# A hybrid DeltaNet, Hyena and expert kernel: its long convolution in 64 real slots, its output weights, expert lists and last norm rearranged

## The chip, the cores and the metric

The kernel runs on one core of one Trainium2 chip, in one launch, with all of its data in f32. The time is that of the device, in microseconds (us), from the launch's first instruction to its last. Of the kernel before there are three timed runs: 4009.3, 4010.4 and 4012.45 us, median 4010.4. One more execution was profiled.

## What is computed

The reference is one layer over 2048 latent tokens of width 1024 and 256 context tokens. Cut to what matters:

```python
hc = rmsnorm(ctx, norm1_g) * (1 + sc1c) + sh1c
_, s_f, s_b = deltanet_branch(hc @ w_in[:, :A_COLS], lp, s0, s0, None)
hx = rmsnorm(x, norm1_g) * (1 + sc1x) + sh1x
p = hx @ w_in
ya = deltanet_branch(p[..., :A_COLS])            # bidirectional gated delta rule, width 512
yb = hyena_branch(p[..., B_OFF:C_OFF])           # long convolution, 256 channels
yc = shortconv_branch(p[..., C_OFF:G_OFF])
gates = sigmoid(p[..., G_OFF:])
merged = gates[0]*(ya @ w_a) + gates[1]*(yb @ w_b) + gates[2]*(yc @ w_c)
x = x + g1x * (merged @ w_out)
h = rmsnorm(x, norm2_g) * (1 + sc2x) + sh2x
x = x + g2x * expert_choice_moe(h)               # 16 experts, each takes its 256 best tokens
return rmsnorm(x, final_norm_g)

# in hyena_branch, with l = 2048 and a filter of 4096 taps for each channel:
y = irfft(rfft(z, n=2*l) * rfft(kern), n=2*l)[:l]
y = x0 * (y + z * hy_d_bias)
```

## The kernel before

The kernel is a sequence of blocks. In a block each engine has its own list of instructions, ordered by hand, and the engines meet at semaphores; all of them meet at a block's end. Some tiles live on through several blocks. SP's queue does most loads and stores, and it works its list in order, so a load that waits holds the loads behind it. Most products over 1024 rows are done two by two blocks with seven products instead of eight (`product`, `into`, `onto`), for which VectorE makes sums of the weights (S1 to S4) and of the activations (T1 to T4).

The blocks that the change touches, in the order of time, by their lines:

- L1120 to L1519, DeltaNet's chunked recurrence. It reads and writes its chunks through SP's queue.
- L1532 to L1932, the projection for Hyena and the short convolution: 12 products of 256 columns of `w_in` (`raw_h`, two buffers), for two halves of the tokens. The first two buffers are loaded at the block's start (`load_raw(0)`, `load_raw(1)`).
- L1942 to L2001, the convolution's first transform. 4096 points are taken as 64 times 64. For each of the 64 residues of the position (a slot) one table of 66 columns (real and imaginary parts of 33 frequencies) is the weight; the moving operands are the filter (`hb`, 512 columns, both directions) and the signal (`zb`, 256 columns). A table has entries only in one group of 32 rows in four. The results go to `fa_d` in HBM: 3 planes of 2x33x64x256.
- L2015 to L2166, the second transform, the product of the spectra and the way back, in 22 parts (`PARTS`) of 384 columns. Each part takes two products of the signal, four of the filter, two products on VectorE, a sum on GpSimd and one product back, which is stored in `fb_d`. Beside it the two DeltaNet outputs (`of_d`, `ob_d`) of 16 token tiles are loaded, added on GpSimd, squared on ScalarE and normed on VectorE.
- L2171 to L2252, the last transform, again in 64 slots, with tables `fd` of 66 rows padded by zeros (two memsets), and DeltaNet's outputs transposed and multiplied by `szb`. The result `y_d` goes to HBM.
- L2259 to L2294: `y_d` is loaded, transposed and gated.
- L2299 to L2559, the gates and the branches' products: 24 quads (`quads`), 12 for each half of the tokens. The first `raw_w` and `bw` are loaded at the block's start. VectorE's order has slots after each quad.
- L2573 to L2889, the output projection. `wo` (4 MB) and the modulation rows `mods` are loaded; VectorE multiplies the weights by g1x (`weighted`, L2722, four times 128x2048) and makes T1, T2, T4 and one more sum of them; then 8 steps (m) of 256 tokens, with residual, norm, transposes and router. The tokens' half of `hT` is dead in the second half of the block before, but isn't used.
- L2897 to L3557, the experts. The 256th best score of each expert is found by 30 votes (L3028 to L3035); `slots` (L3049 to L3065) gives each chosen token its place; `one_hot` (L3073, L3075) and `lists` (L3375, 16 products) make the lists of 8 experts at a time, `listed` (L3083 to L3089) turns them into row numbers, and GpSimd gathers the rows (L3495). Lists 0 to 7 come before the first tokens are turned (L3388), lists 8 to 15 between the turn and the first product. The lists' scratch is the fourth weight buffer, so the load of the fourth matrix (n == 3) waits for both.
- The end of that block: in the last expert's three products the 16 token tiles are loaded (`load_tokens`), squared on ScalarE (`root`) and normed, five of them on GpSimd (`ON_POOL`, L3543 and L3545) and eleven on VectorE (`normed`, L3168). The last expert's rows are added, normed and scattered (`rows`, L3237, L3240, L3554).

## Time and profile before

| | us |
|---|---|
| three timed runs | 4009.3, 4010.4, 4012.45 |
| the profiled execution | 4010.63 |
| its span | 4008.8 |
| granted TensorE clock, mean | 0.967 |

| block (us from the span's start) | length | TensorE busy | DMA share |
|---|---|---|---|
| first transform (1591.1 to 1696.4) | 105.3 | 85.66 | 0.67 |
| second transform (1696.4 to 1816.6) | 120.2 | 103.28 | 0.87 |
| last transform (1816.6 to 1875.0) | 58.4 | 40.76 | 0.64 |
| gates (1889.4 to 2699.7) | 810.3 | 799.43 | 0.17 |
| output projection, first step (2699.7 to 2747.9) | 48.2 | 27.09 | 0.69 |
| votes and lists (2969.7 to 3061.2) | 91.5 | 38.01 | 0.35 |
| experts (3061.2 to 3920.6) | 859.4 | 859.40 | 0.60 |
| last expert and last norm (3920.6 to 4008.8) | 88.2 | 59.28 | 0.63 |

The times of a profile are those of one execution. A busy TensorE is not one at its peak, since its instructions overlap. A matrix product of this program on f32 stands in the trace as two records for each instruction of the kernel.

### The profile page before, as it was taken

To read this page: it belongs to the slowest core of one execution; us is meant where nothing else is said; L and a number is where in the kernel's file an instruction comes from. 1 tells how busy PE (TensorE), PEld (TensorE's weight loads), DVE (VectorE), ACT (ScalarE), POOL (GpSimd) and SP (SyncE) were. 2 spreads that over 40 slices of the span, in tenths; PEclk is the share of its full clock that TensorE was granted. 3 is DMA by queue.
4 is the path that set the end of the run, shared out by engine and by line. 5 is a ranking of instruction groups with operands and counts; after the bars stand their busy time and mean duration, and the time that the engine had idled before them with its cause. 6 is when DMAs were issued, how large, how long until landed. Compare 5 with 4: busy or idle time off the path is not lost. (4 is left out here: it accounts for less than half of the span.)

```text
span 4008.8 us, 46525 instructions
## 1 busy us (share of the span) xinstructions
PE 3710.6 (93%) x17010; PEld 2345.9 (59%) x17010; DVE 1940.5 (48%) x2964; ACT 1104.3 (28%) x2318; POOL 900.3 (22%) x661
## 2 busy tenths in 40 slices
PE   6899997999998998896999999988976999999997
PEld 2355445888886443353444444434546877887785
DVE  4344644555555653645222322214345666566657
ACT  4265654444444411040111111111211111111113
POOL 1022223333333500041011111112331121212124
PEclk9999999999999999998999999999978999999998
DMA  7132323222223511695111111115433655665565
GB/s 269 46 87 79 87 84 100 79 78 78 78 78 101 167 43 56 205 252 160 40 53 53 53 53 53 53 51 184 158 148 109 207 190 191 223 207 191 190 221 208
DMA packets 297696, 497.23 MB, mean 124 GB/s; under 512 B 21447, under 2 KB 176746, under 8 KB 297204
## 3 DMA queue, kind: packets, MB, share of 16 engines
q1 hardware_dynamic: 277601, 431.65, 32.6%
q0 software_dynamic: 12096, 43.84, 4.2%
q10 hardware_dynamic: 7829, 19.46, 1.5%
q8 instruction: 108, 1.77, 0.2%
q14 instruction: 62, 0.51, 0.0%
HBM read 384.11 MB, written 110.77 MB: 123 GB/s over the span
## 5 line engine op out<-in xcount | busy, mean ns | idle before, releaser
L2367 PE MATMUL bank<-hT,raw_w 128*128 128x512 f32 x576 | 261.2, 596 | 10.3 <-DMA raw_w<-in_w_in 10.3
L3396 PE MATMUL bank<-xeT,raw_e 128*128 128x128 f32 x2304 | 267.8, 275 | 0.0
L3396 PEld LDWEIGHTS bank<-xeT,raw_e 128*128 128x128 f32 x2304 | 263.6, 192 | 7.2 <-issue 7.2
L2559 POOL TENSOR_TENSOR mg<-mg,sg_m 128x512 f32<-128x512 f32 x64 | 88.1, 1377 | 720.0 <-DVE sg_m L2461 720.0
L938 POOL TENSOR_SCALAR sg<-tmp 128x512 f32<-128x512 f32 (+1 forms) x76 | 113.4, 1492 | 434.9 <-DVE tmp L1006 374.8
L2367 PEld LDWEIGHTS bank<-hT,raw_w 128*128 128x128 f32 x576 | 110.2, 191 | 149.2 <-issue 138.7
L3396 PE MATMUL bank<-T_e,U 128*128 128x128 f32 x1536 | 176.7, 275 | 0.0
L3396 PEld LDWEIGHTS bank<-T_e,U 128*128 128x128 f32 x1536 | 174.1, 192 | 0.0
L2367 PE MATMUL bank<-zT,S 128*128 128x512 f32 x384 | 172.6, 592 | 0.0
L666 PE MATMUL bank<-T_d,S_d 128*128 128x512 f32 x384 | 171.5, 593 | 0.0
L2461 DVE TENSOR_TENSOR sg_m<-sg_m,bank 128x512 f32<-128x512 f32 x64 | 43.9, 686 | 242.2 <-PE bank L2379 242.2
L2430 ACT ACTIVATE sg_m<-sg_m 128x512 f32<-128x512 f32 x72 | 45.3, 630 | 395.3 <-DVE sg_m L2470 395.3
L1264 PE MATMUL bank<-T,Nc 128*128 128x128 f32 x864 | 137.1, 281 | 15.0 <-DVE T L1464 11.9
L1274 PE MATMUL bank<-E,TTm 128*128 128x128 f32 x864 | 146.6, 294 | 0.2
L1487 DVE TENSOR_TENSOR E<-bank,lv 128x256 f32<-128x256 f32 x216 | 91.6, 424 | 82.7 <-PE bank L1264 82.1
L1274 PEld LDWEIGHTS bank<-E,TTm 128*128 128x128 f32 x864 | 113.4, 191 | 27.0 <-issue 3.8
L3402 PE MATMUL bank<-raw_e,hid_e 128*128 128x512 f32 x288 | 128.9, 592 | 0.0
L1264 PEld LDWEIGHTS bank<-T,Nc 128*128 128x128 f32 x864 | 114.6, 192 | 20.9 <-issue 17.9
L2367 PEld LDWEIGHTS bank<-zT,S 128*128 128x128 f32 x384 | 73.0, 190 | 91.8 <-issue 91.8
L666 PE MATMUL bank<-hT,raw_d 128*128 128x512 f32 x256 | 118.0, 604 | 6.8 <-DMA raw_d<-in_w_in 6.8
L1348 ACT ACTIVATE Tq<-T 128x256 f32<-128x256 f32 x216 | 89.1, 420 | 122.2 <-DVE T L1496 73.5
L666 PEld LDWEIGHTS bank<-T_d,S_d 128*128 128x128 f32 x384 | 71.7, 190 | 85.5 <-issue 85.4
(512 smaller groups left out, 7555.2 us busy)
## 6 DMA issues: line engine op xcount, KB each, us to landing
raw_e<-in_exp_w_gate SPq DMA_DIRECT2D x16, 3072.0 KB, 16.5
raw_e<-in_exp_w_up SPq DMA_DIRECT2D x16, 3072.0 KB, 12.4
raw_e<-in_exp_w_down SPq DMA_DIRECT2D x16, 3072.0 KB, 10.2
raw_w<-in_w_in SPq DMA_DIRECT2D x24, 1024.0 KB, 5.5
raw_d<-in_w_in SPq DMA_DIRECT2D x16, 1024.0 KB, 5.7
fa_d<-az ACTq DMA_DIRECT2D x48, 264.0 KB
sp_in<-fa_d SPq DMA_DIRECT2D x66, 192.0 KB, 4.8
raw_h<-in_w_in SPq DMA_DIRECT2D x12, 1024.0 KB, 5.4
```

Source lines behind the costliest of these rows:

```text
L666: mm = pe.matmul(bank[:, :], lhs[:, k, :], rhs[:, k, :], start=first and k == 0, stop=k == 3, skip_group_check=not first)
L938: pool.tensor_scalar_max(sg[:, g % TB, 0:w], tmp[:, g % TB, 0:w], CLAMP).then_inc(clamp_ok, 1)
L1264: last = pe.matmul(b4(x)[:, h % 2, :], Nc[:, h, :], mixed(T, b, h, 1, 0), start=True, stop=True)
L1274: last = pe.matmul(b4(2 + x)[:, h % 2, :], TTm[:, h, :], E1[:, h, :], start=True, stop=True)
L1348: act.activation(Tq[:, 2 * x:2 * x + 2, :].rearrange("p h (n t b) -> p (h n) t b", t=2, b=b), mixed(T, b, 2 * x, 2, 1), ACT.Copy).then_inc ...
L1487: dve.tensor_tensor(E1[:, 2 * x:2 * x + 2, :], b4(x)[:, 0:2, :], lv[:, l, :].unsqueeze(1).to_broadcast([P, 2, P]), ALU.mult).then_inc(P_ok, 1)
L2367: mm = pe.matmul(bank[:, :], lhs[:, k, :], rhs[:, k, :], start=first and k == 0, stop=k == 3, skip_group_check=not first)
L2430: act.activation(sg[:, i, :], src, ACT.Sigmoid).then_inc(sg_ok[i], 1)
L2461: dve.tensor_tensor(dst, sg[:, i, :], O(q, i)[:, :], ALU.mult).then_inc(pr_ok[i], 1)
L2559: pool.tensor_tensor(mg[:, i, :], mg[:, i, :], sg[:, i, :], ALU.add).then_inc(add_ok[i], 1)
L3396: mm = pe.matmul(bank[:, f * P:(f + 1) * P], lhs[:, k, f * P:(f + 1) * P], rhs[:, k, :], start=fresh and k == 0, stop=k == 3, skip_group_c ...
L3402: mm = pe.matmul(bank[:, :], lhs[:, f, :], rhs[:, f, :], start=first and f == 0, stop=f == HF - 1, skip_group_check=not first)
```

## The change

1. Long convolution. Every slot now holds two residues that lie 32 apart: 32 pairs with tables of 128 columns (32 real frequencies, two parts, two residues), made so that frequency 0 and frequency 32, both real, share one place. The filter is 256 columns of two stacked directions, and the signal 256. The planes in HBM become `fa_d` (2, 32, 2, 64, 256) and `fb_d` (32, 2, 64, 256). The second transform has 16 parts of 512 columns: one product of the signal, two of the filter, two products on VectorE, and two accumulating products back; GpSimd's sum is gone. The last transform has 8 blocks of 4 pairs; its tables need no padding.
2. What blocks need first is loaded in the block before: `raw_h` and the tables `gm` at the start of the recurrence, the first filter and table in the last quad of the projection, `fd` at the end of the second transform, `raw_w` and `bw` in the block that gates `y_d`.
3. Output weights. `w_out`, g1x and the first tokens are loaded in the second pass of the gates' block, into dead parts of `hT`, `x0T` and `ycT`; VectorE weights them and makes three of the four sums there, one such operation after each of seven quads (`prepared`).
4. Lists. The lists of experts 0 and 1 are made first (`early_one_hot`, `early_list`, with 32 of 128 rows and columns). The other two sets of lists are made beside expert 0: their 16 products each stand after the first product and after the gate of expert 0.
5. Last norm. All 16 tiles are normed on VectorE. The last expert's down projection is done in four places with eight products (`last_down`), without sums, each place added to its rows on VectorE.

The core of the diff:

```diff
-FK = FN // 2 + 1
+FK = FN // 2
+PAIRS = FN // 2
+BLOCKS = [b for m in range(4) for b in (m, m + 4)]
-    fa_d = scr("fa_d", (3, 2, FK, FN, HW))
-    fb_d = scr("fb_d", (2, FN, FK, HW))
+    fa_d = scr("fa_d", (2, FK, 2, FN, HW))
+    fb_d = scr("fb_d", (FK, 2, FN, HW))
...
+                    for q in range(2):
+                        c0 = B_OFF + q * HW
+                        sp.dma_start(raw_h[:, q], A["w_in"][0, :, c0:c0 + HW].rearrange("(k p) c -> p k c", p=P)).then_inc(raw_h_in, 16)
+                    sp.dma_start(gm[:, :, :], A["t_g"]).then_inc(g_in, 16)
...
+                    def signal(o, j):
+                        return pe.matmul(PS[(NB * o + j) % 8][:, 0:HW], table(o, 0, j), zb[:, o // 2, j, :], start=True, stop=True)
+                    def filtered(o, j):
+                        return pe.matmul(PS[(NB * o + j) % 8][:, HW:2 * HW], table(o, 1, j), filters(o)[:, j, :], start=True, stop=True)
...
+                    for o in range(NBLK):
+                        b = BLOCKS[o]
+                        act.wait_ge(a_ev, NB * (o + 1))
+                        for s in range(2):
+                            act.dma_start(fa_d[s].rearrange("k r (i m) c -> (k r i) m c", i=2)[:, NB * b:NB * (b + 1), :], az[:, o % RA, s]).then_inc(a_st[o % RA], 16)
...
+                        for s, done in ((0, s_in), (1, hz_in)):
+                            sp.dma_start(sp_in[:, n % RS, s], fa_d[s, 2 * n:2 * n + 2].rearrange("k r n c -> (r n) k c")).then_inc(done[n % RS], 16)
...
+                        for c, g in columns(m):
+                            pe.matmul(PS[6 + v][:, c], gm[:, g + 3, :], yp[:, v, 0, c], start=True, stop=False)
+                            last = pe.matmul(PS[6 + v][:, c], gm[:, g + 4, :], yp[:, v, 1, c], start=False, stop=True)
...
+                        if q == QP + 1:
+                            w_out = A["w_out"][0].rearrange("(k p) c -> p k c", p=P)
+                            sp.wait_ge(o_mm, 4 * QP)
+                            sp.dma_start(g1b, mod_d[:, 0:D].to_broadcast([P, D])).then_inc(g1_in, 16)
+                            for c in range(2):
+                                sp.dma_start(wo[:, :, c * 512:(c + 1) * 512], w_out[:, :, c * 512:(c + 1) * 512]).then_inc(wo_in[c], 16)
...
                         if q >= 1:
                             gated(q - 1, 3)
+                        prepared(q - QP - 2)
...
-                            sp.wait_ge(slots_ok, 2)
+                            sp.wait_ge(slots_ok, 3)
...
                         into(X(n), w(n, 0, 0), t(0, 0), True).then_inc(p1_mm, 1)
+                        if n == 0:
+                            list_of(0)
...
                     for e in range(NE):
                         gate_or_up(3 * e)
+                        if e == 0:
+                            list_of(1)
...
+                        normed(5, 6, 7)
+                        dve.wait_ge(ye_st, 32 * LAST)
+                        dve.wait_ge(rows_in, 32)
+                        onto_rows(0)
+                        normed(8, 9, 10)
+                        onto_rows(1)
+                        normed(11, 12, 13)
+                        onto_rows(2)
+                        normed(14, 15)
+                        rows(1)
+                        onto_rows(3)
+                        rows(0)
```

## Rows read from the trace of the kernel before

**Rows 1.** The page, part 1: busy time, share of the span, instructions.
```profile
PE 3710.6 (93%) x17010; PEld 2345.9 (59%) x17010; DVE 1940.5 (48%) x2964; ACT 1104.3 (28%) x2318; POOL 900.3 (22%) x661
```

**Rows 2.** Busy times by stretch: PE, PEld, DVE, ACT, POOL, granted clock, DMA share, GB/s.
```profile
1591.10:1696.40 105.30, 85.66 (x256) 35.25 (x256) 62.08 (x96) 0.00 (x0) 0.00 (x0) 0.94 0.67 204
1696.40:1816.60 120.20, 103.28 (x308) 59.25 (x308) 47.15 (x76) 44.42 (x115) 47.67 (x38) 0.93 0.87 227
1816.60:1875.00 58.40, 40.76 (x192) 19.88 (x192) 34.60 (x49) 0.00 (x0) 1.80 (x1) 0.85 0.64 174
...
1889.40:2699.70 810.30, 799.43 (x1856) 353.22 (x1856) 192.94 (x272) 103.93 (x169) 88.14 (x64) 0.99 0.17 52
2699.70:2747.90 48.20, 27.09 (x57) 11.34 (x58) 26.20 (x20) 4.72 (x8) 5.11 (x3) 0.77 0.69 241
...
3061.20:3920.60 859.40, 859.40 (x5911) 708.74 (x5911) 534.20 (x554) 134.13 (x256) 170.30 (x131) 1.00 0.60 200
3920.60:4008.80 88.20, 59.28 (x379) 46.30 (x377) 65.59 (x49) 33.64 (x89) 42.04 (x19) 0.86 0.63 227
```

**Rows 3.** The same view where the DMA engines are busy throughout.
```profile
1720.00:1750.00 30.00, 30.00 (x94) 17.59 (x93) 12.38 (x22) 12.78 (x32) 14.78 (x14) 1.00 1.04 280
...
3940.00:3950.00 10.00, 10.00 (x92) 10.00 (x92) 5.57 (x5) 7.35 (x19) 0.51 (x1) 1.00 1.02 414
```

**Rows 4.** First transform: timeline (start, length, engine, line), then its copies by form.
```profile
1599.11 1.97 PE L1972 MATMUL bank<-hb,fw 128*66 128x512 f32 x2 [15.15 <-DMA fw<-in_t_fa]
...
1607.20 1.02 PE L1972 MATMUL bank<-hb,fw 128*66 128x512 f32 x2
1608.06 0.59 PE L1973 MATMUL bank<-zb,fw 128*66 128x256 f32 x2
...
L1988 DVE COPY az<-bank 66x512 f32<-66x512 f32 x64 | 43.3, 685 | 37.5 <-PE bank L1972 28.3 <-DMA fa_d<-az 8.8
```

**Rows 5.** Second transform: timeline of its first product, and one group by form.
```profile
1706.44 1.62 PE L2076 MATMUL bank<-sp_in,gm 128*128 128x384 f32 x2 [16.92 <-DMA sp_in<-fa_d]
...
L2082 PE MATMUL bank<-sp_in,gm 128*128 128x384 f32 x44 | 17.8, 486 | 0.0
```

**Rows 6.** Last transform: timeline of its first products, and line L2213: least, median, greatest ns.
```profile
1827.82 2.77 PE L2213 MATMUL bank<-bb,fd 128*32 128x256 f32 x6 [14.97 <-DMA fd<-in_t_fd]
...
L2213 PE MATMUL bank<-bb,fd x128: 376/379/634, 1827.8 to 1868.9; 128*32 128x256 f32 x128
```

**Rows 7.** Timeline at the start of the projection and of the gates' block.
```profile
1267.07 2.29 DVE L1862 TENSOR_TENSOR T_h<-hT 128x2048 f32<-128x2048 f32 x1 [4.00 <-PEq L144]
...
1272.47 6.47 PE L1642 MATMUL bank<-hT,raw_h 128*128 128x512 f32 x8 [10.12 <-DMA raw_h<-in_w_in]
...
1894.85 5.90 PE L2367 MATMUL bank<-hT,raw_w 128*128 128x512 f32 x8 [10.31 <-DMA raw_w<-in_w_in]
```

**Rows 8.** Output projection: timeline, and line L2722 (least, median, greatest ns).
```profile
2717.56 5.84 PE L2649 MATMUL bank<-wo,mt 128*128 128x512 f32 x8 [22.40 <-DVE wo L2722]
...
2747.86 3.60 PE L2649 MATMUL bank<-wo,mt 128*128 128x512 f32 x8
...
L2722 DVE TENSOR_TENSOR wo<-wo,mods x4: 2283/2287/2292, 2715.1 to 2728.2; 128x2048 f32<-128x2048 f32 x4
```

**Rows 9.** Timeline of the first lists.
```profile
3030.60 3.60 DVE L3073 SCALAR_TENSOR_TENSOR raw_e<-raw_e,rt 128x128 f32<-128x128 f32 x16
...
3036.38 5.25 PE L3375 MATMUL bank<-raw_e 128*128 128x128 f32 x32 [10.08 <-DVE raw_e L3075]
...
3043.41 0.18 POOL L3491 COPY idc<-idxP 128x2 uint32<-128x2 uint32 x1 [48.23 <-DVE idxP L3089]
```

**Rows 10.** Timeline of the last expert and the end.
```profile
3950.13 6.22 DVE L3168 SCALAR_TENSOR_TENSOR raw_e<-raw_e,sf,fgb 128x1024 f32<-128x1024 f32 x2
...
3968.87 8.24 PE L3402 MATMUL bank<-U,H 128*128 128x512 f32 x12 [5.95 <-DVE H L3188]
...
3995.64 1.28 DVE L3240 SCALAR_TENSOR_TENSOR ye<-ye,sr,fgb 128x1024 f32<-128x1024 f32 x1
...
3999.55 0.97 POOL L3554 DMA_INDIRECT out_x<-ye,idc  x1 [0.30 <-issue]
```

More of the change, by code:

```diff
@@ new lines, in shape_tables @@
+    m, q = np.arange(PAIRS)[None, :], row % FN
+    kept = lambda t: np.where(t[..., None] % FN == m[..., None] + PAIRS * i2, weights(t), 0.0)
+    fa = np.stack([kept(FR // 2 * row + m % 16), kept(np.where(row < FN, FR * q + m, (n - FR * q - -m % PAIRS) % n))], 1)
+    fa = fa.reshape(P, 2, PAIRS // NB, NB, P)[:, :, BLOCKS].transpose(0, 2, 1, 3, 4)
+    a2 = np.arange(FN)
+    t = FR * a2[None, :] + m.T
+    k3, s3 = k[:, None, None], s[:, None, None]
+    fd = np.where(s3 == 0, np.cos(angle(k3, t)), np.where(k3 == 0, even(t), -np.sin(angle(k3, t))))
@@ new lines, in shape_tables @@
+    none, last = np.zeros((FN, FK)), np.where(n2 % 2 == 0, 1.0, -1.0)
+    second = lambda x: np.concatenate([last, x[:, 1:]], 1)
+    p_z = top([e0.real, none, second(e0.imag), none], [none, e1.real, none, e1.imag])
+    p_r = top([e0.real, none, second(e0.real), none], [none, e1.real, none, e1.real])
+    p_i = top([e0.imag, none, e0.imag, none], [none, e1.imag, none, e1.imag])
+    alone = np.where(row % FN == 0, 0.0, 1.0)
+    p_inv = p_z.T * (1 + alone)
+    gm = np.stack([top([gr, gi], [-gi, gr]), top([gr, gr], [-gi, -gi]), top([gi, gi], [gr, gr]), inv, turned(inv),
+                   p_z, p_r, p_i * alone.T, p_inv, turned(p_inv) * alone], 1)
@@ L2002, in build @@
+                    for r in range(RA):
+                        act.wait_ge(a_st[r], 32 * len(range(r, NBLK, RA)))
+        hst.close()
         if stop == 8:
             return
-        CW = 3 * HW // 2
+        CW = 2 * HW
         TILES = SEQ // P
@@ L2069, in _ @@
+                        last.then_inc(c_mm, 1)
                     for m in range(PARTS):
-                        n, v = m // 2, m % 2
-                        if v == 0:
-                            pe.wait_ge(s_in[n % 2], 96 * (n // 2 + 1))
-                        sig = [sp_in[:, n % 2, s].rearrange("p k c -> p (k c)")[:, v * CW:(v + 1) * CW] for s in range(3)]
-                        if m >= 1:
-                            pe.wait_ge(sx_cp, 2 * m)
-                        pe.matmul(PS[0][:, 0:CW], gm[:, 0, :], sig[0], start=True, stop=True)
@@ L2077, in _ @@
-                        pe.matmul(PS[1][:, 0:CW], gm[:, 1, :], sig[0], start=True, stop=True).then_inc(sx_mm, 1)
+                        v, r = m % 2, m % RS
+                        sig = [sp_in[:, r, s].rearrange("p k c -> p (k c)") for s in range(2)]
+                        pe.wait_ge(s_in[r], 16 * (m // RS + 1))
+                        if m >= 2:
+                            pe.wait_ge(sx_cp, m - 1)
+                        for c, g in columns(m):
+                            last = pe.matmul(PS[v][:, c], gm[:, g, :], sig[0][:, c], start=True, stop=True)
@@ L2083, in _ @@
-                        pe.matmul(PS[3 + 2 * v][:, 0:CW], gm[:, 5, :], sig[2], start=False, stop=True).then_inc(sx_mm, 1)
+                        for c, g in columns(m):
+                            pe.matmul(PS[2 + v][:, c], gm[:, g + 1, :], sig[1][:, c], start=True, stop=True)
+                            last = pe.matmul(PS[4 + v][:, c], gm[:, g + 2, :], sig[1][:, c], start=True, stop=True)
+                        last.then_inc(f_mm, 1)
                         if m >= 1:
@@ L2203, in _ @@
+                    for b in range(RD):
+                        load(b)
+                    for b in range(NBLK):
+                        if b + RD < NBLK:
+                            load(b + RD)
+                        for t in range(TB * b + 4, TB * (b + 1) + 4):
+                            if t < TILES:
+                                sp.wait_ge(ya_ok, t - 3)
+                                sp.dma_start(szb[:, t % 4], sz_d[t]).then_inc(sz_in[t % 4], 16)
                 @block.tensor
```

763 lines of the change are left out of this document (403 added, 360 removed).

## The prediction

> **What bounds the kernel now.** I read the page's busy times first: TensorE is busy for 93% of the span [rows 1]. A share over the whole span hides which blocks have slack, so I then cut the span at the blocks' bounds. In the gates' block and in the experts TensorE is busy for 799.4 of 810.3 us and 859.4 of 859.4 us at a granted clock of 0.99 and 1.00 [rows 2]: there only less TensorE work would help, and the change takes none away. The time to win lies in three other places. The three blocks of the convolution take 105.3, 120.2 and 58.4 us, 283.9 in all, two of them mostly TensorE work, with the DMA engines at 0.64 to 0.87 [rows 2]. At several blocks' starts TensorE stands still for its first load [rows 4 to 8]. And at the end the chain of work that ended last runs through VectorE, where norms (L3168) and the last expert's sums take turns [rows 10]. So I price each block from its start to the next one's start.
>
> **First transform.** Before, one slot takes 0.86 us for 512 columns and 0.43 for 256, read from start to start (1607.20 to 1608.06 and half as much again) [rows 4]; 64 slots are 82.6 us, which with 8.0 us to the first product (1591.1 to 1599.11) and the wait for the last stores make the 105.3. After, 32 pairs take 256 and 256 columns, 0.86 us each: 27.5 us, or 55 at half the clock. The 32 copies of 512 columns are 32 x 0.685 = 22 us on VectorE [rows 4]. TensorE and VectorE thus both drop out, and the question is what is late next: the transfers. Loads in the block: signal 2.1 MB, seven tables of 0.52 MB, seven filters of 0.52 MB, 9.4 MB in all (the eighth of each comes earlier, at a cost of nothing, since the projection's block has TensorE as its bound and idle DMA engines). Stores: 2 planes x 32 x 2 x 64 x 256 x 4 bytes = 8.4 MB. That is 17.8 MB. At full share the rate was 280 GB/s with pieces of 1 and 2 KB and 414 with pieces of 4 KB [rows 3]; this block before ran 204 at 0.67, or 304 at full share, on a like mixture [rows 2]. I take 310: 57.5 us, and 5 for the first landing and the last stores, 62.5. Gain 42.8. Bounds: 270 GB/s and no better overlap, 71 us (gain 34); 380 GB/s, 52 us (gain 53), under which TensorE at half clock would be the bound in any case.
>
> **Second transform.** One instruction of 384 columns took 0.65 us of TensorE from start to start, two records of 0.486 overlapping [rows 5]; seven in each of 22 parts are 99 us. After, a part is five of 512 columns, 5 x 0.86 = 4.3 us, 16 parts are 69. VectorE has two products of 512 columns (1.4 us) and 22 steps of the norm over 16 parts (about 2.5 us), 3.9 in all, just under TensorE's 4.3; GpSimd's sum and the two semaphores around it go. Transfers: planes 8.4 MB, DeltaNet's outputs 8.4, stores 4.2, `szb` and `fd` 2.1, 23 MB in place of 27. The DeltaNet loads all lie in the first ten parts: up to there 8.4 + 5.2 + 2.1 = 15.7 MB at 280 GB/s [rows 3], 56 us, so those parts wait for transfers, and the last six or seven run at TensorE's pace, 28 us. With 4 us to the first product (before 10, 1696.4 to 1706.44 [rows 5]; the tables are there and the first piece is one DMA instead of six) and 6 for the last product back, copy and store: 94. Gain 26. Bounds: TensorE alone, 69 + 12 = 81 (gain 39); the rings of three instead of four tiles hold SP back, 105 (gain 15).
>
> **Last transform.** The products of 256 columns go from 64 (27.5 us) to 32 (13.8); two records of 0.379 [rows 6]. The 16 groups of transposes stay, 10.6. Transfers are 9.4 MB, now in pieces of 4 KB for the loads: 28.5 us at 330 GB/s, between the two rates of [rows 3]. The two memsets and the wait for `fd` go, which held TensorE from 1816.6 to 1827.8 [rows 6]; 4 us stay for the first load and 4.5 for the last store. 37. Gain 21.4; bounds 15 (270 GB/s) and 25 (engines alone).
>
> **Starts.** In the projection TensorE waited for `raw_h` until 1272.47 while VectorE started at 1267.07 [rows 7]. The gain is at most 5.4 us; ScalarE's copy of the first product stands behind its six scalings of loaded tiles, so the third product will wait some 2 us: 3.6 (bounds 2.5 and 5.4). The moved loads cost SP's queue three issues in the recurrence, behind its first chunks and ahead of its first stores, where the queue has slack. In the gates' block TensorE waited from 1889.4 to 1894.85 [rows 7]: 5.4 (bounds 4 and 5.5); the loads now stand behind those of `y_d` on SP's queue, 3 MB in the 14 us that the block before lasts.
>
> **Output weights.** Before, the first step of the projection took 48.2 us with TensorE busy for 27.1 [rows 2]; its first product waited to 2717.56 for the weighted `wo` [rows 8]. After, all of it is there: 5.8 us for the first product at the low clock, six more of 3.43, some stall, 28. That is 20 less. It costs seven VectorE operations of 2.29 us [rows 8] in a block where VectorE is busy for 193 of 810 us [rows 2]; each stands behind the last gate of a quad, and what is queued behind it is the next quad's first gate. The sums for the next quad are made before it, and the banks are doubled, so I take 1 us for all and 19 as the gain (bounds 3, if each operation stops TensorE, and 20).
>
> **Lists.** Before, one-hot tables (5.8 us from 3030.60), 5.25 us of products at 3036.38 and the rest led to GpSimd's gather at 3043.41 [rows 9]. Digits and tables for two experts are 2.5 and 2 us; the digits of the rest (4 us) stand ahead of the list's reading on VectorE. I put the gather at 3037, 6.4 us earlier. But three lists' products instead of two now stand on TensorE's path (4.6 us more, less a little), the first product starts at a low clock, and only the reading of the second list (2 us) is hidden: net 3 (bounds 0 and 5). The fourth matrix's load waits some 26 us longer than before, to about 3087; it lands near 3100, 2 or 3 us ahead of its first sum.
>
> **The end.** A row norm of 1024 columns took 1.28 us alone [rows 10]; with GpSimd at work two took 6.22 [rows 10]. The Trainium skill explains this (SBUF — State Buffer, on the shared port pair): the pair is an exclusive lock, and the loser waits out the whole instruction. The rows agree. With GpSimd's ten operations gone, 16 norms are 20.5 us. I followed VectorE's list: hidden rows ready at 3957, eight products of 2.57 us on TensorE from 3958 to 3979 without the 5.95 us wait of before [rows 10], the last rows at 3984, all stores landed near 3984. From the last scatter to the end were 8.3 us (4000.5 to 4008.8) [rows 10]: end near 3995. I take 13 (bounds 6, if 8.4 MB of stores in 25 us pile up, and 17).
>
> **The sum.** 42.8 + 26 + 21.4 + 3.6 + 5.4 + 19 + 3 + 13 = 134.2. Made against the profiled execution's 4010.6 (0.2 over the median of the timed runs): 3876.
>
> **Rivals.** (a) The convolution's blocks leave TensorE at its low level, 1.2 GHz of 2.4, because it waits often. For it: the granted clock was 0.85 over the last transform, with waits [rows 2], and the first two records of the first transform took twice the later ones [rows 4]. Against: TensorE stays busy for some 70% of the second transform. Price: 16 x 8.6 + 10 = 148 instead of 94, 57 instead of 37: 3951. (b) Transfers run nearer to 414 GB/s and TensorE is the bound: 52, 81 and 33: 3848. (c) The seven operations in the gates' block stop TensorE each time: 16 us back, 3892. (d) Part of the change does not do what it says: the loads ahead are late or the end stays bound by stores; without starts and end 22 us back, 3898. (e) Slower than before: TensorE, with fewer pauses, is granted less clock in the long blocks. It is busy for some 3600 us; it has to lose 142 us, from a mean clock 3.9% lower on. Against: with no pause at all for 859 us the clock was 1.00 [rows 2]. It would give over 4018. (f) Every transfer of the convolution now steps from partition to partition or plane to plane by powers of two (32 KB, 128 KB), where one layout had 33 rows. If lock-step streams fell on the same channels, and the rate were 207 GB/s, which is just the mean that the first block had already (204 [rows 2]): 50.2 MB in 243 us and 24 for ends, 73 more: 3949. Against: planes with steps of 64 KB moved at 280 [rows 3]. [...]
>
> **How the numbers follow.** Forecast 0.62, (a) 0.08, (b) 0.12, (c) 0.06, (d) 0.07, (e) 0.01, (f) 0.04. The bounds of the terms, taken as independent, give 3859 to 3900 around 3876. Reaching to (b) below and past (c) and (d) above, with their own spread, gives 3848 to 3912. What a measurement can tell from no change is about 0.2%. Only (e) is not faster: faster 0.98, same 0.01, slower 0.01.
>
> **What would show it.** In the new profile: the first transform's block some 62 us long with a DMA share over 0.9 and TensorE busy for half of it; the second 94 us, with waits for `sp_in` in its first ten parts and none after; the first product of the output projection within 1 us of its block's start; seven new VectorE operations of 2.3 us in the gates' second pass and no new wait of TensorE; the gather near 6 us earlier after the votes; L3168's successors at 1.28 us each. Wrong would be: a DMA share under 0.8 in the first transform, a clock of 0.5 through the second, or a wait of TensorE for the fourth expert matrix.

## The result, and the profile after

The changed kernel takes 3857.85 us (median of four runs, 3856.97 to 3861.17), the kernel before 4009.85 us beside it (4007.09 to 4012.45): a ratio of 0.9623, with a 95% interval of 0.9606 to 0.9639, or 152 us less. Forecast were 3876, with 3848 to 3912 as the range. The profiled execution of the changed kernel took 3861.2 us with a span of 3859.4 us, 149.4 less than the span before.

The page after, busy times (answers to [rows 1]). TensorE's instructions are 290 fewer and its busy time 85.6 us less:

```profile
PE 3625.0 (94%) x16720; PEld 2317.5 (60%) x16720; DVE 1868.6 (48%) x2887; ACT 1091.8 (28%) x2281; POOL 850.5 (22%) x625
```

The busy times by stretch (columns as in [rows 2]), with the blocks' bounds found as before by the first DMA issue or first product of each: projection, first, second and last transform; then gates, the first step of the output projection, the votes up to expert 1's first product, and the last expert up to the end.

```profile
1268.58:1589.41 320.83, 305.61 (x721) 135.59 (x721) 173.15 (x194) 90.99 (x140) 82.16 (x56) 0.98 0.30 95
1589.41:1651.14 61.73, 40.02 (x128) 30.63 (x128) 22.14 (x32) 0.00 (x0) 0.00 (x0) 0.78 0.90 289
1651.14:1733.06 81.92, 72.84 (x170) 33.46 (x170) 42.26 (x64) 33.38 (x81) 20.27 (x16) 0.95 0.86 282
1733.06:1768.07 35.01, 25.24 (x128) 15.90 (x128) 21.05 (x32) 0.00 (x0) 0.00 (x0) 0.86 0.78 271
...
1782.97:2589.01 806.04, 800.06 (x1857) 353.48 (x1857) 208.76 (x280) 104.25 (x170) 98.15 (x64) 1.00 0.18 56
2589.01:2616.84 27.83, 26.95 (x56) 11.58 (x57) 10.95 (x13) 4.54 (x8) 5.07 (x3) 0.91 0.60 211
...
2838.80:2984.96 146.16, 97.17 (x589) 81.82 (x590) 87.53 (x330) 12.47 (x22) 30.41 (x20) 0.73 0.39 145
...
3787.04:3859.40 72.36, 58.12 (x384) 46.29 (x383) 44.35 (x46) 32.00 (x86) 8.64 (x6) 0.94 0.76 276
```

Read beside the same view of the kernel before, whose votes up to expert 1 and whose last stretch were:

```profile
2969.73:3118.69 148.96, 95.50 (x555) 80.23 (x556) 83.90 (x311) 12.52 (x22) 30.41 (x20) 0.74 0.38 142
3920.77:4008.80 88.03, 59.11 (x378) 46.14 (x377) 65.59 (x49) 33.64 (x89) 41.87 (x19) 0.86 0.63 227
```

this gives the account of the 149.4 us:

| stretch | before | after | gain | predicted gain |
|---|---|---|---|---|
| up to the projection's first product (1267.07, 1268.58) | | | -1.5 | 0 |
| projection | 324.0 | 320.8 | 3.2 | 3.6 |
| first transform | 105.3 | 61.7 | 43.6 | 42.8 |
| second transform | 120.2 | 81.9 | 38.3 | 26 |
| last transform | 58.4 | 35.0 | 23.4 | 21.4 |
| gating of `y_d` | 14.4 | 14.9 | -0.5 | 0 |
| gates and first step of the output projection | 858.5 | 833.9 | 24.6 | 24.4 (5.4 and 19) |
| votes to expert 1 | 149.0 | 146.2 | 2.8 | 3 |
| last expert and norm | 88.0 | 72.4 | 15.7 | 13 |

The one large difference is the second transform. Its rows show TensorE at work nearly throughout while the DMA engines are full, but at a rate that [rows 3] had not shown for this block:

```profile
1661.00:1671.00 10.00, 10.00 (x28) 5.13 (x27) 4.07 (x7) 4.13 (x8) 4.77 (x4) 1.00 1.10 343
1671.00:1681.00 10.00, 9.70 (x23) 3.90 (x21) 6.07 (x11) 4.24 (x11) 4.29 (x4) 1.00 1.07 343
1681.00:1691.00 10.00, 8.56 (x20) 3.61 (x20) 6.96 (x9) 4.64 (x13) 4.71 (x5) 1.00 1.06 347
1691.00:1701.00 10.00, 8.61 (x20) 3.29 (x19) 6.01 (x10) 4.78 (x13) 4.54 (x4) 1.00 1.08 342
1701.00:1711.00 10.00, 10.00 (x25) 4.44 (x24) 6.97 (x12) 4.83 (x14) 0.40 (x1) 1.00 0.63 209
```

Before, the DMA engines at a share of 1.04 moved 280 GB/s; now, at 1.07, they move 343. TensorE's products of this block waited only 3.1 us for planes after the first one (groups by form, TensorE: busy us, mean ns, idle before and its releaser):

```profile
L2135 PE MATMUL bank<-sp_in,gm 128*128 128x512 f32 x30 | 15.7, 606 | 3.1 <-DMA sp_in<-fa_d 3.1
L2135 PE MATMUL bank<-sp_in,gm 128*128 128x256 f32 x4 | 2.1, 674 | 7.9 <-DMA sp_in<-fa_d 7.9
```

In the gates' block the four weightings and three sums are there, with no idle VectorE before them, and the waits of TensorE from 1782.97 to 2616.84 name none of them: the 5.1 and 2.9 us are the two blocks' starts, one 0.9 us stood in the gates' block before too, and the other is for a sum of the output projection itself (L2806).

```profile
L2586 DVE TENSOR_TENSOR hT<-hT,ycT 128x2048 f32<-128x2048 f32 x4 | 9.1, 2285 | 0.0
...
L2595 DVE TENSOR_TENSOR yaT<-hT 128x2048 f32<-128x2048 f32 x1 | 2.3, 2285 | 0.0
L2599 DVE TENSOR_TENSOR yaT<-hT,yaT 128x2048 f32<-128x2048 f32 x1 | 2.3, 2285 | 0.0
L2601 DVE TENSOR_TENSOR hT<-hT 128x2048 f32<-128x2048 f32 x1 | 2.3, 2285 | 0.0
```

```profile
PE bank L2728 <- PEq L2394: 5.1, 1, 5.1
PE bank L2438 <- PEq L2306: 2.9, 1, 2.9
PE bank L2728 <- DVE hT L2806: 0.9, 1, 0.9
PE bank L2438 <- DVE sg_m L2541: 0.9, 1, 0.9
```

The gather of expert 0's rows starts at 2905.41, 66.6 us after the votes' start (2838.80); before it was 73.7 (3043.41 less 2969.73, [rows 9]), so 7.1 us earlier:

```profile
2905.41 0.19 POOL L3650 COPY idc<-idxP 128x2 uint32<-128x2 uint32 x1 [41.04 <-DVE idxP L3184]
```

At the end the chain that ended last now runs through TensorE until its last product, and only 14 us behind it (start, length, what):

```profile
3787.04 37.52 PE bank L3533 x336
3824.56 20.62 PE bank L3539 x48
...
3845.20 0.76 DVE ye L3312
...
3848.03 1.30 DVE ye L3350
...
3850.15 0.97 POOL out_x L3700
```

### The profile page after: what moved, and what is told of

It is laid out like the page before. It is cut to its first block and busy times, and to the rows that moved or that the text cites. A ratio compares the mean times of both kernels' runs of the same rounds, so it can differ in the third digit from the quotient of the medians.

```text
span 3859.4 us, 45580 instructions
## 1 busy us (share of the span) xinstructions
PE 3625.0 (94%) x16720; PEld 2317.5 (60%) x16720; DVE 1868.6 (48%) x2887; ACT 1091.8 (28%) x2281; POOL 850.5 (22%) x625
## 5 line engine op out<-in xcount | busy, mean ns | idle before, releaser
L2651 POOL TENSOR_TENSOR mg<-mg,sg_m 128x512 f32<-128x512 f32 x64 | 98.2, 1534 | 705.2 <-DVE sg_m L2532 705.2
L3539 PE MATMUL bank<-raw_e,hid_e 128*128 128x512 f32 x318 | 141.6, 592 | 0.0
L1287 PEld LDWEIGHTS bank<-T,Nc 128*128 128x128 f32 x864 | 115.4, 193 | 21.7 <-issue 18.7
L1371 ACT ACTIVATE Tq<-T 128x256 f32<-128x256 f32 x216 | 89.1, 420 | 123.2 <-DVE T L1519 73.7
## 6 DMA issues: line engine op xcount, KB each, us to landing
raw_e<-in_exp_w_down SPq DMA_DIRECT2D x16, 3072.0 KB, 10.2
```

The lines of the kernel that those rows point to most:

```text
L1287: last = pe.matmul(b4(x)[:, h % 2, :], Nc[:, h, :], mixed(T, b, h, 1, 0), start=True, stop=True)
L1371: act.activation(Tq[:, 2 * x:2 * x + 2, :].rearrange("p h (n t b) -> p (h n) t b", t=2, b=b), mixed(T, b, 2 * x, 2, 1), ACT.Copy).then_inc ...
L2651: pool.tensor_tensor(mg[:, i, :], mg[:, i, :], sg[:, i, :], ALU.add).then_inc(add_ok[i], 1)
L3539: mm = pe.matmul(bank[:, :], lhs[:, f, :], rhs[:, f, :], start=first and f == 0, stop=f == HF - 1, skip_group_check=not first)
```

## The experiments

All runs but one are edits of the changed kernel; blocks are read from the trace, each by itself, since all engines meet at a block's end. One number is needed for reading them: the first transform, where a run does not touch it, took 58.9, 59.6, 61.7, 61.7, 62.6 and 65.3 us in six executions. A difference of 3 us there means nothing. The second transform is steadier: five kernels with one and the same code for it took 76.9 to 77.6, and two with that of the changed kernel 81.9 and 81.0. The end is steadier still: in ten kernels with the changed kernel's end it is the same within 0.1 us. Of a_tensor, b_bytes, c_halves, k_whole, g_spread and j_quarters there is one execution each.

**What bounds the three transforms: TensorE's work changed (a_tensor).**

```diff
                             signal(o, j)
+                            filtered(o, j)
                             filtered(o, j).then_inc(a_mm, 1)
...
-                            pe.matmul(PS[6 + v][:, c], gm[:, g + 3, :], yp[:, v, 0, c], start=True, stop=False)
-                            last = pe.matmul(PS[6 + v][:, c], gm[:, g + 4, :], yp[:, v, 1, c], start=False, stop=True)
+                            last = pe.matmul(PS[6 + v][:, c], gm[:, g + 3, :], yp[:, v, 0, c], start=True, stop=True)
...
+                            for again in range(2):
                                 last = pe.matmul(PS[e % 4][0:FN, j % 2 * HW:(j % 2 + 1) * HW], fd[:, NB * b + j, :], bb[:, b % RD, j, :],
...
                         if n == 0:
                             list_of(0)
+                            list_of(1)
```

Not shown in the diff: six of the seven prepared operations are done twice, the additional ones into sums that are written later.

> TensorE work is added or taken in five blocks of the changed kernel, each read on its own in the trace; it leaves the output wrong in the second transform, since the second half of each product back is missing. First transform: each product of the filter is done twice, 32 more of 0.43 us = 13.7 us of TensorE. If transfers bind: block 61.7 -> at most 65; if TensorE binds: 75. Second transform: the second accumulating product back is left out, 16 x 0.86 = 13.8 us less. If TensorE binds: 81.9 -> 70 to 74 (then transfers stop it); if transfers bind: 80 to 82. Last transform: each product twice, 13.8 us more. If TensorE binds: 35.0 -> 46 to 49; if transfers bind: at most 38. Gates' block: six of the seven prepared operations are done twice, 13.7 us more of VectorE. If they are hidden: 805.0 -> at most 806; if each stops TensorE: 819. Lists: the products for the third list stand right behind those for the second, ahead of the rest of expert 0's gate. If the place behind the gate hides VectorE's tables: votes' start to expert 1's first product 146.2 -> 149 to 152; if it hides nothing: 146 to 147.

```profile
1589.00:1653.66 64.66, 50.08 (x192) 41.06 (x192) 21.83 (x32) 0.00 (x0) 0.00 (x0) 0.87 0.88 276
1653.66:1727.81 74.15, 59.56 (x136) 26.90 (x136) 44.14 (x64) 33.73 (x81) 20.56 (x16) 0.94 0.96 312
1727.81:1775.32 47.51, 39.69 (x192) 24.93 (x192) 21.45 (x32) 0.00 (x0) 0.00 (x0) 0.90 0.64 200
1789.79:2595.51 805.72, 799.74 (x1856) 353.33 (x1857) 226.11 (x286) 104.17 (x170) 98.10 (x64) 1.00 0.18 57
```

First transform: 64.7, inside the untouched runs' scatter, though TensorE was busy for 10 us more: TensorE does not bind it. Last transform: 12.5 us longer for 13.7 us of products: TensorE binds it. Second: 7.8 us shorter for 13.8 us less. The DMA share rose from 0.86 to 0.96, and TensorE's waits for planes behind the first product grew from 3.1 to 8.1 us. So TensorE binds it, with the transfers close behind. The gates' block did not get longer (806.0 before the edit, 805.7 with it) although VectorE was busy for 17.3 us more: the slots behind each quad have room for nearly twice the work. The lists were a miss in size: from expert 0's turn to expert 1's first product 81.6 us in place of 71.3, so the place behind the gate hides 10.2 us, not 3 to 6. TensorE waited 6.75 us for VectorE's tables there, and its 32 products of the third list then took 6.74 us where those of the second, behind other work, took 3.74.

**The same from the other side: bytes taken away (b_bytes).**

```diff
-            filters = lambda o: (filter0, other[:, 0], other[:, 1], hb[:, :, :])[o % 4]
+            filters = lambda o: filter0
-                        load_filter(sp, filters(o), BLOCKS[o], h_in[o % 4])
...
-                        sp.dma_start(obb[:, t % RO], o_d[1][CTX // P + t]).then_inc(o_in[t % RO], 16)
...
-                                sp.dma_start(szb[:, t % 4], sz_d[t]).then_inc(sz_in[t % 4], 16)
```

> Transfers are taken away in three blocks of the changed kernel (so its output is wrong: one filter piece serves for all, the second DeltaNet output is not read, and 12 of 16 gate tiles are not loaded). First transform: 7 filters less, 3.7 MB of 17.8. If transfers bind: 3.7 MB at 310 GB/s = 12 us less, 61.7 -> 50; if not: 60 to 62. Second transform: 4.2 MB of 23 less. If TensorE binds: 81.9 -> 78 to 80, only its few waits for planes go; if transfers bind: 4.2 MB at 343 GB/s = 12 less, 70. Last transform: 3.1 MB of 9.4 less. If TensorE binds: 35.0 -> 33 to 35; if transfers bind: 26.

```profile
1586.98:1626.97 39.99, 30.16 (x128) 25.08 (x128) 20.23 (x32) 0.00 (x0) 0.00 (x0) 0.88 0.91 355
1626.97:1704.88 77.91, 71.90 (x170) 34.12 (x170) 40.84 (x64) 33.26 (x81) 17.18 (x16) 0.94 0.76 243
1704.88:1738.58 33.70, 25.90 (x128) 16.39 (x128) 21.64 (x32) 0.00 (x0) 0.00 (x0) 0.85 0.61 188
```

The second and last transform answer as TensorE-bound blocks: 4.2 and 3.1 MB taken away gave 4.0 and 1.3 us. The first answers as one that transfers bind, but with nearly twice the expected size: 21.7 us for 3.7 MB, that is 170 GB/s (145 to 195 with the block's scatter). These loads are the ones of 64 partitions, one of 256 KB and four of 64 KB for each filter.

**Why 343 GB/s and not 280: loads of 64 partitions (c_halves, k_whole).** The kernel before loaded each plane of the second transform in DMAs of 64 partitions, the changed one in DMAs of 128. The first run puts the halves back; it also puts back the loads made ahead for the projection and the gates.

```diff
-                            sp.dma_start(sp_in[:, n % RS, s], fa_d[s, 2 * n:2 * n + 2].rearrange("k r n c -> (r n) k c"))...
+                            for r in range(2):
+                                sp.dma_start(sp_in[r * FN:(r + 1) * FN, n % RS, s], fa_d[s, 2 * n:2 * n + 2, r].rearrange("k n c -> n k c"))...
```

> In the second transform each load of a plane's part is made by two DMAs of 64 partitions, as before the change, in place of one of 128. If the DMAs' form is why 343 GB/s moved at full share where the kernel before moved 280: the rate falls to about 280, the first ten parts wait, and the block goes from 81.9 to 92 or 96, near the 94 of the prediction. If the layout or the mixture is the reason: 81 to 84. The loads made ahead for two blocks are put back at their blocks' starts: the projection should start its first product 4 to 5 us later and be 3.2 longer (320.8 -> 324), the gates' block should go from 805.0 to 810; if those loads were hidden anyway: no change.

The second run has the same number of DMAs, of the same 128 KB and the same 1 KB pieces, but each goes to all 128 partitions:

```diff
+                            for k in range(2):
+                                sp.dma_start(sp_in[:, n % RS, s, k], fa_d[s, 2 * n + k].rearrange("r n c -> (r n) c"))...
```

> The changed kernel, each load of a plane's part in the second transform made by two DMAs as in the run with halves (four DMAs of 128 KB a part, 1 KB pieces), but each DMA goes to all 128 partitions and takes one of the two frequencies, where that run's took 64 partitions and both. There the block went from 81.9 to 93.8 us and the rate at full share from 344 to 287 GB/s. If a fixed cost of each DMA did that: 91 to 95 us again. If it is that a DMA writes 64 partitions only: 80 to 84 us and 330 to 350 GB/s.

The second transform's block with the halves, by stretch:

```profile
1654.92:1748.76 93.84, 74.66 (x170) 32.05 (x170) 40.13 (x64) 33.96 (x81) 21.75 (x16) 0.96 0.85 246
```

The same with DMAs to all 128 partitions:

```profile
1653.66:1736.32 82.66, 73.03 (x170) 33.12 (x170) 42.34 (x64) 33.30 (x81) 20.27 (x16) 0.95 0.88 280
```

And a stretch of 30 us within it, with the halves:

```profile
1665.00:1695.00 30.00, 23.27 (x55) 9.49 (x54) 11.97 (x19) 11.18 (x27) 10.65 (x8) 1.00 1.06 287
```

with all 128 partitions:

```profile
1665.00:1695.00 30.00, 27.52 (x63) 11.16 (x61) 16.38 (x25) 12.93 (x31) 13.04 (x11) 1.00 1.06 338
```

and in the changed kernel itself:

```profile
1665.00:1695.00 30.00, 27.57 (x64) 11.49 (x63) 17.50 (x25) 14.03 (x35) 13.08 (x12) 1.00 1.07 343
```

At the same DMA share of 1.06, with the planes loaded by 64 partitions, the rate is 287 GB/s and the block takes 93.8 us, the predicted 94; the same number of DMAs of the same size to 128 partitions gives 338 and 82.7. So with these pieces of 1 KB neither their size, nor the number of DMAs, nor the layout in HBM made the old rate, but that half of the partitions were written by each. All these rates are of mixtures: in the 30 us with the halves the planes' loads were 2.7 of 8.6 MB. If the other 5.9 MB moved at 338, the halves themselves moved at some 215 GB/s (an estimate from these rows). TensorE's waits for planes went from 11.0 us to 20.9 with the halves and to 11.5 without.

The loads put back at the blocks' starts cost 3.0 us in the projection (its first product waited 10.02 us instead of 4.75, at 1274.64; the block ended 318.5 us later instead of 320.8) and 5.5 in front of the gates (20.4 us from the first load of `y_d` to the gates' first product instead of 14.9, with 10.67 us of wait for `raw_w`). Predicted were 3.6 and 5.4.

**Do the DeltaNet loads hold the first parts up (g_spread, g_timed)?**

```diff
-                        for t in (2 * n - 3, 2 * n - 2):
+                        for t in range(3 + (n - 3) * 11 // 8, 3 + (n - 2) * 11 // 8):
```

> The DeltaNet outputs of the second transform are loaded 11 tiles in 8 parts instead of 2 in each part. If TensorE's waits for planes in the first ten parts come from these loads' share of the DMA engines: the waits (some 4 us) go, the block goes from 81.9 to 77 to 79. If the waits come from the ring of three tiles or from the latency of each load: 81 to 82.

> The spread loads again, with timed rounds. By its trace the first look was 10.6 us shorter than the changed kernel's profiled run, 4.7 of it in the second transform, 2.1 in the first transform, which is not touched. If the 4.7 us are the edit's and the rest is scatter between executions: median 3852 to 3855 against 3858.

```profile
1649.01:1726.21 77.20, 70.96 (x170) 33.30 (x170) 42.40 (x64) 33.27 (x81) 20.72 (x16) 0.96 0.92 300
```

The block takes 77.2 us in g_spread (77.6 in g_timed), and TensorE's waits for planes are down to 0.3 us behind the first product. The one execution of g_spread took 3850.66 us, the four of g_timed 3854.08 in the median (3848.99 to 3856.4), 3.8 less than the changed kernel. Their ratio to the kernel before is 0.9602 (0.9586 to 0.9618) and overlaps the changed kernel's, so it is the trace that shows this gain. The mechanism of the prediction's first ten parts was right; what it cost was 4 to 5 us, not 13.

**The filters in DMAs of 128 partitions (h_filters, i_rows), and more DMAs of the same bytes (j_quarters).** The two directions of a filter's slot stand at a fixed distance in HBM, so one DMA can fetch both.

```diff
-                eng.dma_start(buf[0:64], rows[:, NB * b:NB * (b + 1), 0:HW]).then_inc(done, 16)
                 for j in range(NB):
-                    eng.dma_start(buf[64:P, j, :], rows[:, -(NB * b + j) % PAIRS, HW:2 * HW]).then_inc(done, 16)
+                    m = NB * b + j
+                    near, away = m * 2 * HW, -m % PAIRS * 2 * HW + HW
+                    both = bass.AP(h_d.tensor, h_d.offset + min(near, away), [[abs(away - near), 2], [PAIRS * 2 * HW, 64], [1, HW]])
+                    eng.dma_start(buf[:, j, :], both).then_inc(done, 16)
```

That is h_filters. In i_rows the first two steps of the source change places, `[[PAIRS * 2 * HW, 64], [abs(away - near), 2], [1, HW]]`, and the rows of the filter's table with them.

> The changed kernel with the spread loads of the run before, and each filter of the first transform loaded by four DMAs of 128 partitions and 1 KB pieces in place of one DMA of 64 partitions and four of 64 (the two directions stand at a fixed distance in HBM, so one DMA can take both; where the second comes first the table's rows change places). Bytes and 1 KB pieces stay as they are. Without the filters the block took 40.0 us instead of 61.7, 22 us for 3.7 MB. If the 64 partitions are the cost, as in the second transform: 61.7 -> 50 to 56 us, and the time 3858 -> 3840 to 3846 with the 5 to 7 us of the spread loads. If the 1 KB pieces are the cost: 59 to 62, and 3850 to 3852.

Far slower: 3917.65 us (3916.97 to 3920.76), and the block took 127.5 us. Where only filter loads run, the share is that of hardly more than two of the 16 DMA engines:

```profile
1588.51:1716.00 127.49, 47.14 (x128) 35.68 (x128) 21.85 (x32) 0.00 (x1) 0.00 (x0) 0.67 0.40 140
...
1623.00:1629.00 6.00, 3.06 (x7) 2.52 (x8) 0.69 (x1) 0.00 (x0) 0.00 (x0) 0.50 0.15 50
```

> The spread loads, and each filter by four DMAs of both directions as in the run before, but now the source's outermost step is the 64 rows and the two directions are the next one, so that SBUF's rows take the directions by turns (and the table's rows with them). The run before had the two directions outermost, and its filter loads moved 45 GB/s with 1 to 2 of 16 DMA engines busy: first transform 59.6 to 61.7 -> over 110 us. If DMA engines take their share by the outermost step: all 16 are busy again and the block is back at 62 us or less. If each DMA has a fixed cost of some 0.34 us of all 16 engines (35 DMAs and 3.7 MB less gave 21.8 us, of which 9 are the bytes at 414 GB/s; in the second transform twice the DMAs gave 12), 28 DMAs in place of 35 give 2.4 us more: 57 to 60 us. If the number of partitions of a DMA is what costs: 52 to 56. The time 3848 to 3851.

With the 64 rows outermost instead of the two directions, and the same bytes in the same pieces, the block's DMA share is back at 0.86:

```profile
1590.03:1645.20 55.17, 36.99 (x128) 29.30 (x128) 21.56 (x32) 0.00 (x0) 0.00 (x0) 0.81 0.86 324
1645.20:1722.55 77.35, 71.47 (x170) 33.96 (x170) 42.44 (x64) 33.28 (x81) 20.83 (x16) 0.95 0.92 299
```

Ten of its microseconds at full share (of their 4.13 MB, 2.90 were the stores of `fa_d`):

```profile
1620.00:1630.00 10.00, 3.76 (x17) 3.06 (x17) 2.85 (x5) 0.00 (x0) 0.00 (x0) 0.95 1.04 413
```

The block takes 55.2 us, 3.7 below the shortest of the six untouched ones, and the median is 3845.53 us (3842.8 to 3848.23), a ratio of 0.9580 to the kernel before with an interval of 0.9564 to 0.9596, wholly below the 0.9606 at which the changed kernel's begins. This is the fastest version found, 12.3 us under the changed kernel. The 55.2 lie in the range expected from partitions and under the 57 to 60 of a fixed cost of each DMA, though it is one execution of a block that scatters. What SP's queue held of the DMA engines says the same without that scatter. Over this block (58.9 us in g_timed, 55.2 in i_rows) it moved the same 9.44 MB in both, but took these shares of the 16 engines (packets, MB, share):

```profile
q1 hardware_dynamic: 5728, 9.44, 59.6%
q1 hardware_dynamic: 5616, 9.44, 48.4%
```

That is 35.1 us of all engines in g_timed and 26.7 in i_rows, 8.4 less, of which the block gave back 3.7. The form of the filters' loads is thus not all of their 21.7 us: with 128 partitions the block is still 15.2 us longer than without them (40.0, b_bytes).

In j_quarters the filters are loaded as in the changed kernel, and the tables in quarters:

```diff
-                        sp.dma_start(fw[:, o - 1], A["t_fa"][:, o]).then_inc(fw_in[o], 16)
+                        for u in range(4):
+                            sp.dma_start(fw[32 * u:32 * u + 32, o - 1], A["t_fa"][32 * u:32 * u + 32, o]).then_inc(fw_in[o], 16)
```

> The spread loads, and each of the seven tables of the first transform is loaded by four DMAs of 32 partitions in place of one of 128: 21 DMAs more, the same bytes in the same pieces of 4 KB. If a DMA has a fixed cost of some 0.34 us: 60 to 62 -> 67 to 69 us in the first transform. If only small pieces cost: 60 to 62, no change.

62.6 us, against 58.9 and 59.6 of the kernels that it was made from: at most 3.7 us for 21 DMAs, not 7, and inside the scatter of the untouched block. A fixed cost of 0.34 us each is refuted, a smaller one is not. The run says something else too: these tables went to 32 partitions at a time, in pieces of 4 KB, and lost no more than that. A loss by writing few partitions is therefore shown for pieces of 1 KB only (planes and filters); no run varies the two separately.

**The end: norms or down projection (d_pool_norm, e_before_norm).** The first gives five norms back to GpSimd in the changed kernel; the second takes all norms to VectorE in the kernel before.

```diff
 d_pool_norm (changed kernel)
+            ON_POOL = (2, 4, 6, 9, 11)
+                    for i, tile in enumerate(ON_POOL):
+                        pool.tensor_tensor(tokens(tile), tokens(tile), sf[:, tile, :].to_broadcast([P, D]), ALU.mult)...
+                        pool.tensor_tensor(tokens(tile), tokens(tile), fgb[:, :], ALU.mult)...
 e_before_norm (kernel before)
-            ON_POOL = (2, 4, 6, 9, 11)
+            ON_POOL = ()
-                            normed(5, 7, 8, 10, 12)
+                            normed(5, 6, 7, 8, 9, 10, 11, 12)
```

> The changed kernel with five of the 16 last norms on GpSimd again (tiles 2, 4, 6, 9, 11), the down projection with eight products kept. If GpSimd's row operations hold VectorE up (two norms took 6.22 us in the kernel before): norms beside them take 2 to 3.4 us, and the stretch from the last expert's gate to the end goes from 72.4 to 76 to 80 us, the time from 3858 to 3862 to 3866. If the gain at the end came from the down projection alone: 72 to 73 us, no change.

> The kernel before with all 16 last norms on VectorE, the down projection with seven products and its sums kept. If the norms on GpSimd were the greater part of what the end lost: the stretch from the last expert's gate to the end goes from 88.0 to 78 to 82 us, the time from 4010 to 4001 to 4004. If the sums of the down projection were: 85 to 88 us, 4007 to 4010. With the other half of the pair, the two edits' gains should add up to 15.7 us if they are independent.

The stretch from the last expert's gate to the end in d_pool_norm:

```profile
3785.01:3862.90 77.89, 58.36 (x384) 46.36 (x383) 51.80 (x41) 32.00 (x86) 35.44 (x16) 0.91 0.71 257
```

And in e_before_norm:

```profile
3922.78:3999.70 76.92, 55.78 (x378) 45.07 (x377) 54.48 (x54) 33.63 (x89) 15.05 (x9) 0.89 0.72 260
```

| the end's length | norms shared with GpSimd | norms on VectorE |
|---|---|---|
| down projection with seven products | 88.0 (before) | 76.9 |
| down projection with eight products | 77.9 | 72.4 (after) |

Each of the four lengths is from one execution; against the 0.1 us of scatter at this end the differences are clear. Taken first, the norms give 11.1 us and the down projection then 4.5; the other way round the down projection gives 10.1 and the norms then 5.5. The two edits overlap: both take work from the same chain through VectorE, and once TensorE sets the pace (58.1 of 72.4 us busy) more room on VectorE buys nothing. The norms' own rows show what GpSimd does to them. In the changed kernel:

```profile
L3268 DVE SCALAR_TENSOR_TENSOR raw_e<-raw_e,sf,fgb 128x1024 f32<-128x1024 f32 x12 | 15.1, 1280 | 6.3 <-ACT sf L3417 6.2
```

In d_pool_norm, with the additions to the last rows and GpSimd's own second operation:

```profile
L3275 DVE SCALAR_TENSOR_TENSOR raw_e<-raw_e,sf,fgb 128x1024 f32<-128x1024 f32 x8 | 17.4, 2199 | 7.6 <-ACT sf L3424 7.6
...
L3353 DVE TENSOR_TENSOR ye<-ye,xe 128x512 f32<-128x512 f32 x4 | 5.0, 1260 | 0.1
...
L3707 POOL TENSOR_TENSOR raw_e<-raw_e,fgb 128x1024 f32<-128x1024 f32 x4 | 11.7, 2914 | 0.3
```

The means mix two cases. Of the eight norms three ran while GpSimd computed nothing, at 1.27 to 1.29 us as in the changed kernel; the five beside GpSimd took 1.65 us and more, 2.7 in the mean. Of the four additions the two beside GpSimd took 1.60 and 2.06 us, the other two 0.69. Operations that take one input from a TensorE bank kept their time beside the same GpSimd instructions: 0.54 us for 128x384 at 3816.62 (L3240), 0.56 alone at 3795.76. In time the first run is at 3861.82 us (3861.03 to 3864.65), 4.0 over the changed kernel's median; their ratios to before have the same interval (0.9606 to 0.9639), so only the trace shows this difference clearly. The second is at 4000.65 us (3997.2 to 4004.36), a ratio of 0.9969 (0.9957 to 0.9982) to the kernel before.

## Why the prediction was right, and where a term was off

- **First transform, 62.5 against 61.7.** Right, and for the reason given: transfers bind (a_tensor, b_bytes), share 0.90, TensorE busy for 40 of 61.7 us. The 310 GB/s were a good mean of two unlike parts: the seven filters at some 170, everything else at 355 (b_bytes). That loads to half of the partitions cost more was not in the working, and it is only a part of the filters' cost (i_rows). The exact hit is luck by some 3 us, since the block itself scatters from 58.9 to 65.3.
- **Second transform, 94 against 81.9: the mis-sized term.** The failing step is "15.7 MB at 280 GB/s, 56 us, so those parts wait for transfers". The 280 of [rows 3] was the rate of loads of 64 partitions. At the rate measured after, 343, the 15.7 MB take 46 us, almost TensorE's 43 for ten parts, and the waits for planes behind the first product were 3.1 us where the working had 13 (56 less 43). With the old form of the loads they are 12.2 and the block takes 93.8 (c_halves), so the rest of that working fits in sum. TensorE's own bound, set at 81, was too high by 3 us or more: with 0.3 us of waits the block took 77.6 (g_timed), and its two ends in c_halves were 3.5 and 3.3 us, not 4 and 6. The row was taken for a property of the pieces' size; the two layouts stood in the diff, and asking what else differed between the old and new loads would have moved the term towards its bound.
- **Last transform, 37 against 35.0.** The sum assumed that 28.5 us of transfers bind. They do not: TensorE does (a_tensor), from 1736.70 on without a wait, with 3.6 us ahead and 6 behind. Both ways give nearly the same length.
- **Starts, 3.6 and 5.4 against 3.0 and 5.5** when undone by themselves (c_halves).
- **Output weights, 19.** Gates and first step together gained 24.6 of the predicted 24.4. The first step is 27.8 us (28 predicted). The seven operations cost nothing that can be seen, and six more did not either; the 1 us set for them and rival (c), 16 us, are refuted.
- **Lists, 3 against 2.8.** The gather was 7.1 us earlier (6.4), the three lists' products took back most of it, and no wait for the fourth matrix is in the trace. Not foreseen: putting the third list behind the gate saves 10 us against putting it ahead; the working had counted only that 2 us of a reading are hidden.
- **End, 13 against 15.7.** The norms take 1.28 us as predicted and TensorE has no wait of 5.95 us any more. Its last product ended 58.2 us behind the last gate (3845.2 less 3787.04), just as written (3979 less 3920.77). What followed took 14.2 us where 16 had been laid out (3979 to 3995), and the sum had been rounded down by another 0.8. Not foreseen was that the two edits overlap, each worth 10 or 11 us alone.
- **Rivals.** (a) TensorE at 1.2 GHz: the granted clock was 0.78, 0.95 and 0.86 in the three blocks; no. (b) TensorE-bound in all three: true of two (81.9 and 35.0 against its 81 and 33), false of the first (61.7 against 52), which is why the time lies between the forecast and its 3848. (d) Nothing came late. (e) The gates' block kept a clock of 1.00. (f) No loss from powers of two: 289 GB/s at a share of 0.90 in the first transform, and 413 at 1.04 in i_rows, where 2.90 of 4.13 MB were stores with a step of 32 KB from partition to partition. Its 207 GB/s leaned on the first block's 204 before, but that was at a share of 0.67, 304 at full share. The Trainium skill (DMA: Bandwidth & Descriptors, Latency and other measured facts) lists row pitches from 512 KiB up and has 164 GB/s per direction and less from 2 MiB on; the steps here are below all of them.

By medians the kernel gained 152.0 us against 134.2 forecast; 12.3 of the difference is the second transform, 2.7 the end and 2.0 the last transform, and the rest lies in small terms and in the scatter between executions.

Open: why the first transform's length varies by 6 us from run to run with the same code, whether each DMA has a small fixed cost beside that of half partitions, and whether half partitions cost anything with pieces of 4 KB.

## What to carry to other kernels

A DMA rate read from a trace belongs to the form of the DMAs that made it: before it prices a changed block, compare how many partitions each DMA writes and what its outermost step is, not only bytes and piece size. In a block that transfers bind, look for loads that write only half of the partitions in small pieces; here changing those, with the bytes as they were and 28 DMAs in place of 35, took away 8.4 us of DMA time and some 4 us of the block's length. The two medians lie 8.5 us apart (3854.08 and 3845.53), but their ratios' intervals overlap. Where two edits shorten the same chain, their gains do not add: price the second from what is late once the first is made.

## What the runs showed of the hardware

- With pieces of 1 KB and DMAs of 128 KB, a stretch at a full DMA share (1.06) moved 287 GB/s where the planes' loads wrote 64 partitions each, and 338 where as many loads wrote 128 (c_halves, k_whole). Loads of tables to 32 partitions in pieces of 4 KB cost at most 3.7 us for 3.7 MB (j_quarters).
- Where DMAs whose source has 2 as its outermost step ran alone, the share was 0.15, that of about two of 16 DMA engines, at 50 GB/s. With 64 as the outermost step the block with the same bytes had a share of 0.86, and took 55.2 us in place of 127.5 (h_filters, i_rows).
- GpSimd's row operations hold VectorE's up: 1.28 us alone and 1.65 or more, 2.7 in the mean, beside them for the same 128x1024 instruction; 0.69 and 1.60 to 2.06 for an addition of 128x512. VectorE's operations with one input from a bank are not held up (0.54 us beside, 0.56 alone). The Trainium skill (SBUF — State Buffer, Who interferes with whom) has a VectorE instruction with two SBUF inputs contend with a GpSimd instruction that reads SBUF. The trace agrees: the norms and additions have both inputs in SBUF (d_pool_norm).
